# Moving the norm-factor multiply of tiles 1 to 3 from VectorE to GpSimd at the edge between two layers

## The chip, the cores and the metric

The kernel runs on one core of a Trainium2 chip. The metric is the device time of one launch in microseconds, and the time of a kernel is the median over its runs. Beside the runs there is one profiled execution; every row shown below is of that one.

## What is computed

A decoder trunk of two layers over 512 tokens of width 1024. Each layer normalises its input, runs three mixers (Mamba-2 SSD, latent attention, block-sparse attention) over one input projection, adds their output, normalises again and adds a mixture of experts. Only the first norm of a layer matters here:

```python
def _rms(x):
    return (x * lax.rsqrt(jnp.mean(x * x, axis=-1, keepdims=True) + EPS))

hm = rms_norm(x, norm_mix_g[l]) * (1.0 + sc_m) + sh_m
proj = hm @ w_in[l]
```

The kernel folds `norm_mix_g * (1 + sc_m)` into one row of factors, held in all 128 partitions in `mod[:, D:2*D]`. So a row of the norm's result is (x times factors) times rstd plus shift.

## The kernel before, in words

The 512 tokens are T = 4 tiles of 128 rows; `x[:, t, :]` is tile t, 128 partitions by 1024 f32. At the head of each layer `mixer_rows` (VectorE) makes the normed rows tile by tile. For a tile t the work is handed over as follows:

- ScalarE squares tile t and sums the squares along the row (`x_squares`, L1416, semaphore `xss`). In its own program this stands behind the copies of the columns of tile t-1 (`columns_out`, L1436).
- GpSimd makes rstd of the sum in two tiny instructions, a tensor_scalar (L2441) and a power (L2442), with a wait between them, and raises `xrs`.
- VectorE multiplies the tile by the factors into `x_scaled` (L1875, which is the whole buffer `gain`), once the row of t-1 that read this buffer is done (`hrow_dn`), and then, when `xrs` is up, makes the row: `x_scaled` times rstd plus shift (L1882, raises `hrow_dn`).
- TensorE turns the row into columns (L891), ScalarE copies them out of PSUM rounded to fp32r (L1436), and VectorE takes what the rounding left (`h_low`, L1841). TensorE then multiplies the tile with the first block of input weights (L953). It turns the columns of tile t+1 in the middle of tile t's 24 matmuls, so the rows of the next tile are wanted early.

After tile 3 the further blocks of the projection (L951, L953) follow without a break, whose first operand is all columns of all four tiles.

At the head of the second layer the tiles of x aren't final yet. VectorE adds what the experts gave: `added` (L1767, two of 128x512 for a tile, PSUM and x) and `chosen_added` (L1782, 128x1024, two for a tile, with gathered rows in SBUF and x). In `mixer_rows` these stand between the steps above: for a tile t, `added` of tile t+2, the multiply of tile t, the first `chosen_added` of tile t+1, the row of tile t, the second `chosen_added` of t+1, and `h_low` of t. ScalarE's squares of a tile wait for the second `chosen_added` of it.

GpSimd's own program has nothing else in this stage, apart from the gathers of chosen rows ahead of tile 0 in the second layer, and a memset and one DMA behind tile 3 in the first. Its loop over the tiles before the change is:

```python
for t in range(T):
    g.wait_ge(*at(L, xss, t + 1))
    rstd(rs_x[:, t:t + 1], ss_x[:, t:t + 1], D, xrs)
```

SyncE's loads that hang on this stage are those of the second input block (after row 0) and the first pieces of `ada_w` (after row 2, and after the last transposed columns).

Of the kernel before, what the change touches and what calls it, by code (L numbers as in the profile page):

```python
# [24 lines left out]
ALU = mybir.AluOpType  # L25
# [3 lines left out]
S, D, DEPTH = 512, 1024, 2  # L29
# [83 lines left out]
def trunk(nc, A, out, cpack, bucket_oh, relv, hf_rows, y_rows, mod_rows):  # L113
# [4 lines left out]
    def sb(name, shape, dt=F32):  # L118
        address[name] = -(-nc.sbuf_base // 32) * 32
        return ctx.enter_context(nc.sbuf_tensor(name, shape, dt))  # L120
# [5 lines left out]
    def sem(name, count=0):  # L126

        sems.append(ctx.enter_context(nc.semaphore(name)))
        per_layer[sems[-1].num] = count
        return sems[-1]  # L130

    def at(layer, sem_, n):

        assert n == 0 or per_layer[sem_.num] >= n
        return sem_, n + layer * per_layer[sem_.num]


    x = sb("x", [P, T, D])
    mod = sb("mod", [P, 6 * D])
# [75 lines left out]
    def h_row(base, t):  # L215
        return hfrow[:, t, :] if base else hrow[:, t % 2, :]
# [13 lines left out]
    x_scaled = gain[:]  # L230
# [128 lines left out]
    g_used = sem("gain_used", 5)  # L359
    hrow_dn = sem("h_row_done", 12)  # L360
# [342 lines left out]
    if True:  # L703
        with nc.Block() as block:
# [1056 lines left out]
            def _(v):  # L1761
# [7 lines left out]
                def added(L, t):  # L1769

                    for b in range(2):
                        v.wait_ge(ov_pe[L], TOKEN_ORDER.index((b, t)) + 1)
                        add_by_token(0, b, t).then_inc(x_added, 1)

                def chosen_added(L, t, j):

                    if j == 0:
                        v.wait_ge(*at(L, x_added, 2 * t + 2))
                        v.wait_ge(*at(L, cg[t], 32))
                    else:  # L1780
                        v.wait_ge(vch, step.n)
                    ins = v.scalar_tensor_tensor(x[:, t, :], chosen[:, 2 * t + j, :], w12[:, j, t:t + 1],  # L1782
                                                 x[:, t, :], ALU.mult, ALU.add)
                    if j:
                        ins.then_inc(cdn, 1)
                    else:
                        ins.then_inc(vch, 1)
                        step.n += 1

                def layer(L):  # L1790
# [46 lines left out]
                    def h_low(t):  # L1837

                        for j in range(2):
                            v.wait_ge(*at(L, h_ev, 2 * t + j + 1))  # L1840
                            v.tensor_tensor(hL[:, 4 * j:4 * j + 4, P * t:P * t + P],  # L1841
                                            h_bank(0, t, j)[:, :].rearrange("p (k n) -> p k n", k=4),
                                            actT_r[:, 4 * j:4 * j + 4, P * t:P * t + P].bitcast(F32), ALU.subtract
                                            ).then_inc(hl_dn, 1)

                    def in_weights_lo(i, halves=(0, 1)):
                        for half in halves:
                            raw, lo, hi = in_part(IN_ORDER[i], half)
                            v.wait_ge(*at(L, in_w_hi, 2 * i + half - 1))
                            v.tensor_tensor(lo, raw, hi.bitcast(F32), ALU.subtract).then_inc(in_w_lo, 1)  # L1850
# [9 lines left out]
                    def mixer_rows():  # L1860

                        g_ = mod[:, D:2 * D]
                        if L:
                            added(L - 1, 0)
                            added(L - 1, 1)
                            chosen_added(L - 1, 0, 0)
                            chosen_added(L - 1, 0, 1)
                        for t in range(T):
                            if L:
                                v.wait_ge(*at(L - 1, cdn, t + 1))  # L1870
                                if t + 2 < T:
                                    added(L - 1, t + 2)
                            if t:
                                v.wait_ge(*at(L, hrow_dn, t))
                            v.tensor_tensor(x_scaled, x[:, t, :], g_, ALU.mult).then_inc(g_used, 1)  # L1875
                            if L and t < T - 1:
                                chosen_added(L - 1, t + 1, 0)
                            v.wait_ge(*at(L, xrs, t + 1))
                            v.wait_ge(*at(L, g_used, t + 1))
                            if t >= 2:  # L1880
                                v.wait_ge(*at(L, h_ps, 2 * (t - 1)))
                            v.scalar_tensor_tensor(h_row(0, t), x_scaled, rs_x[:, t:t + 1], mod[:, 0:D], ALU.mult, ALU.add  # L1882
                                                   ).then_inc(hrow_dn, 1)
                            if L and t < T - 1:
                                chosen_added(L - 1, t + 1, 1)
                            if t == T - 1:
                                in_weights_lo(1, halves=(0,))
                            h_low(t)

                    def ffn_rows():  # L1890
# [6 lines left out]
                        for t in range(T):  # L1897
# [13 lines left out]
                            if t < T - 1:  # L1911
                                w_out_add(t + 1, 1)

                    mixer_rows()
                    in_weights_lo(1, halves=(1,))

# [255 lines left out]
                    for n in range(4 * T, 8 * T):  # L2172
                        h, t = n // T, n % T
# [261 lines left out]
            def _(g):  # L2435
                step = Counted(g, gch)
                def layer(L):

                    def rstd(dst, src, width, done):

                        step(g.tensor_scalar(dst, src, 1.0 / width, EPS, ALU.mult, ALU.add))  # L2441
                        g.tensor_tensor(dst, dst, cst[:, C_HALF:C_HALF + 1].to_broadcast(list(dst.shape)), ALU.pow  # L2442
                                        ).then_inc(done, 1)
# [7 lines left out]

                    for t in range(T):
                        g.wait_ge(*at(L, xss, t + 1))
                        rstd(rs_x[:, t:t + 1], ss_x[:, t:t + 1], D, xrs)

                    if L == 0:
# [162 lines left out]
                for L in range(DEPTH):  # L2619
                    layer(L)  # L2620
# [31 lines left out]
```

## Time and profile before

| | us |
|---|---|
| median of 3 runs | 1408.68 |
| lowest and highest run | 1405.8 and 1413.34 |
| profiled execution, its time | 1411.56 |
| profiled execution, its span | 1409.7 |
| TensorE busy in the span | 1312.8 (93%) |
| VectorE busy | 1130.7 (80%) |
| ScalarE busy | 731.6 (52%) |
| GpSimd busy | 237.3 (17%) |

The span is what the profile shows of the program from its first to its last record; 1.86 us of the execution's time lie around it. The mean granted clock of TensorE was 0.972 of full speed. Busy shares are averages over stages: which engine sets the time at the head of a layer has to be read from the timeline of that stage.

### The profile page before, as it was taken

What the parts mean: (1) busy time and instruction counts of PE and PEld (TensorE: products, weight loads), DVE (VectorE), ACT (ScalarE), POOL (GpSimd) and SP (SyncE); (2) the same over time, 40 slices, a digit from 0 to 9 for tenths busy, and PEclk for the clock granted to TensorE, in tenths of its full rate; (3) what the DMA queues carried; (4) which work ended last, traced back from release to release, by engine and by line L of the source; (5) the groups of instructions that cost most, each with busy time, mean ns of one, the idle gap of its engine ahead of it and who ended that gap; (6) DMA issues with size and microseconds to landing.
All of it is one profiled execution on the core that took longest, in us unless ns stands there. A gap on an engine that the chain in (4) does not pass through costs nothing.

```text
span 1409.7 us, 16989 instructions
## 1 busy us (share of the span) xinstructions
PE 1312.8 (93%) x6515; PEld 1045.8 (74%) x6515; DVE 1130.7 (80%) x1335; ACT 731.6 (52%) x963; POOL 237.3 (17%) x293
## 2 busy tenths in 40 slices
PE   6799988879989999999999998988998999999995
PEld 3677766667878888888877777666777888888883
DVE  3679867875579999999886998475557999999986
ACT  1424334562337777777624343447223877777760
POOL 0100136431011000000030013445101100000002
PEclk9899998999999999999999999899999999999998
DMA  9686621433579999999766583010347999999965
GB/s 358 244 297 216 224 94 61 149 119 121 212 292 360 411 409 409 406 407 411 263 229 209 171 277 124 1 60 1 150 173 286 369 403 408 401 415 406 405 238 194
DMA packets 90147, 365.93 MB, mean 260 GB/s; under 512 B 5785, under 2 KB 10631, under 8 KB 80464
## 3 DMA queue, kind: packets, MB, share of 16 engines
q1 hardware_dynamic: 67584, 298.71, 55.7%
q0 software_dynamic: 14160, 51.43, 9.4%
q10 hardware_dynamic: 8320, 14.68, 3.0%
q8 instruction: 53, 0.87, 0.2%
q14 instruction: 30, 0.25, 0.1%
HBM read 336.18 MB, written 28.61 MB: 259 GB/s over the span
## 4 chain that ended last, share of the span: by engine, by line
PE 76%; DVE 10%; issue 4%; ACT 3%; POOL 2%; DMA 2%; DVEq 0%; ACTq 0%; POOLq 0%
PE ps L953 9%; PE ps L1302 8%; PE ps L1304 8%; PE ps L1303 8%; PE ps L951 6%; PE ps L1330 4%; PE ps L1331 4%; PE ps L1332 4%; PE ps L1224 2%; PE ps L1226 2%; PE ps L1225 2%; PE ps L1288 2%; PE ps L1095 1%; PE ps L1126 1%; PE ps L920 1%
## 5 line engine op out<-in xcount | busy, mean ns | idle before, releaser
L1302 PE MATMUL ps<-mod_rounded,work_rounded 128*128 128x512 f32 x340 | 136.9, 403 | 1.8 <-DVE work_rounded L2345 1.8
L1304 PE MATMUL ps<-mod_rounded,work_rounded 128*128 128x512 f32 x340 | 134.6, 396 | 0.0
L1303 PE MATMUL ps<-ring_rounded,work_rounded 128*128 128x512 f32 x288 | 113.9, 396 | 0.0
L2204 DVE TENSOR_TENSOR ring_rounded<-ring,mod_rounded 128x2048 fp32r<-128x2048 f32 (+1 forms) x54 | 102.8, 1929 | 1.4
L1303 PE MATMUL ps<-work_rounded 128*128 128x512 f32 x256 | 101.0, 395 | 0.0
L2204 DVE TENSOR_TENSOR work_rounded<-work,mod_rounded 128x2048 fp32r<-128x2048 f32 (+1 forms) x48 | 91.3, 1930 | 10.0 <-ACT mod_rounded L1680 8.8
L2587 POOL DMA_INDIRECT work<-ffn_rows,slot_idx x34 | 42.0, 1235 | 302.0 <-PE ps L1288 269.3
L953 PE MATMUL ps<-ring_rounded,actT_rounded 128*128 128x512 f32 (+2 forms) x256 | 91.1, 356 | 0.0
L1680 ACT ACTIVATE mod_rounded<-ring 128x2048 fp32r<-128x2048 f32 (+1 forms) x54 | 85.9, 1626 | 0.0
L1812 DVE SCALAR_TENSOR_TENSOR gain<-ring,csil,gain 128x512 f32<-128x512 f32 x106 | 80.8, 763 | 3.0
L1700 ACT ACTIVATE work_rounded<-ps 128x512 fp32r<-128x512 f32 x68 | 37.0, 596 | 84.5 <-PE ps L1288 84.5
L1304 PE MATMUL ps<-actT_rounded,work_rounded 128*128 128x512 f32 x204 | 80.4, 394 | 0.0
L1302 PE MATMUL ps<-actT_rounded,work_rounded 128*128 128x512 f32 x204 | 80.1, 392 | 0.0
L953 PE MATMUL ps<-work_rounded,mod_rounded 128*128 128x512 f32 (+2 forms) x192 | 74.3, 387 | 2.4 <-ACT work L1443 1.3
L1680 ACT ACTIVATE mod_rounded<-work 128x2048 fp32r<-128x2048 f32 (+1 forms) x48 | 76.3, 1624 | 0.0
L1302 PEld LDWEIGHTS ps<-mod_rounded,work_rounded 128*128 128x128 f32 x340 | 64.1, 188 | 16.3 <-DVE work_rounded L2345 2.7
L1304 PEld LDWEIGHTS ps<-mod_rounded,work_rounded 128*128 128x128 f32 x340 | 63.9, 188 | 14.8
L2204 DVE TENSOR_TENSOR ring_rounded<-ring,actT_rounded 128x3072 fp32r<-128x3072 f32 x18 | 60.4, 3356 | 12.2 <-ACT actT_rounded L1680 12.2
L953 PE MATMUL ps<-work_rounded,actT_rounded 128*128 128x512 f32 (+2 forms) x192 | 70.0, 365 | 0.0
L2602 POOL DMA_DIRECT2D expert_rows<-work x32 | 18.1, 567 | 298.5 <-DVE work L2339 298.5
L1303 PEld LDWEIGHTS ps<-ring_rounded,work_rounded 128*128 128x128 f32 x288 | 54.3, 189 | 12.5
L2204 DVE TENSOR_TENSOR work_rounded<-work,actT_rounded 128x3072 fp32r<-128x3072 f32 x16 | 53.7, 3358 | 12.3 <-ACT actT_rounded L1680 12.2
(367 smaller groups left out, 3600.9 us busy)
## 6 DMA issues: line engine op xcount, KB each, us to landing
ring<-in_moe_w_up SPq DMA_DIRECT2D x18, 2048.0 KB, 10.7
ring<-in_moe_w_gate SPq DMA_DIRECT2D x18, 2048.0 KB, 10.4
ring<-in_moe_w_down SPq DMA_DIRECT2D x18, 2048.0 KB
work<-in_moe_w_up SPq DMA_DIRECT2D x16, 2048.0 KB, 10.8
work<-in_moe_w_down SPq DMA_DIRECT2D x16, 2048.0 KB, 11.5
work<-in_moe_w_gate SPq DMA_DIRECT2D x16, 2048.0 KB, 10.4
ring<-in_ada_w SPq DMA_DIRECT2D x30, 1024.0 KB, 5.3
expert_rows<-work POOLq DMA_DIRECT2D x32, 512.0 KB, 7.8
```

The costliest lines, as they stand in the source:

```text
L951: mm = pe.matmul(ps[n % 2][:, :], w_[:, P * t:P * t + P], h_, start=first_, stop=last_)
L953: mm = pe.matmul(ps[n % 2][:, 0:wd], h_[:, P * t:P * t + P], w_, start=first_, stop=last_)
L1302: pe.matmul(ps[j][:, :], xl, hi, start=k == 0, stop=False)
L1303: pe.matmul(ps[j][:, :], xh, lo, start=False, stop=False)
L1304: mm = pe.matmul(ps[j][:, :], xh, hi, start=False, stop=k == KD - 1)
L1330: pe.matmul(ps[6 + b][:, :], hl[:, k, :], hi_[:, k - k0, cols], start=k == 0, stop=False)
L1331: pe.matmul(ps[6 + b][:, :], hh[:, k, :], lo_[:, k, cols], start=False, stop=False)
L1332: mm = pe.matmul(ps[6 + b][:, :], hh[:, k, :], hi_[:, k - k0, cols], start=False, stop=k == 3)
L1680: a.activation(buf, slots[3 * odd + j][:, 512 * k0:512 * k1], ACT.Copy).then_inc(w_hi, 1)
L1812: add(v.scalar_tensor_tensor(acc, w, csil[:, k:k + 1], acc, ALU.mult, ALU.add))
L2204: v.tensor_tensor(slots_r[3 * odd + j][:, 512 * k0:512 * k1], slots[3 * odd + j][:, 512 * k0:512 * k1], buf.bitcast(F32), ALU.subtract).th ...
L2587: g.indirect_dma_start(out=dst, out_offset=None, in_=hf_rows, in_offset=bass.IndirectOffsetOnAxis(ap=col, axis=0)).then_inc(sem_, 16)
```

## The change

The multiply of tile 0 stays on VectorE. For tiles 1, 2 and 3 it is taken out of VectorE's program together with its wait for the row before, and put into GpSimd's loop, behind the wait for the squares and ahead of rstd. It happens at the head of both layers. Buffers, semaphores and counts are the same.

```diff
@@ -1870,9 +1870,8 @@
                                 v.wait_ge(*at(L - 1, cdn, t + 1))
                                 if t + 2 < T:
                                     added(L - 1, t + 2)
-                            if t:
-                                v.wait_ge(*at(L, hrow_dn, t))
-                            v.tensor_tensor(x_scaled, x[:, t, :], g_, ALU.mult).then_inc(g_used, 1)
+                            if t == 0:
+                                v.tensor_tensor(x_scaled, x[:, t, :], g_, ALU.mult).then_inc(g_used, 1)
                             if L and t < T - 1:
                                 chosen_added(L - 1, t + 1, 0)
                             v.wait_ge(*at(L, xrs, t + 1))
@@ -2451,6 +2450,9 @@
 
                     for t in range(T):
                         g.wait_ge(*at(L, xss, t + 1))
+                        if t:
+                            g.wait_ge(*at(L, hrow_dn, t))
+                            g.tensor_tensor(x_scaled, x[:, t, :], mod[:, D:2 * D], ALU.mult).then_inc(g_used, 1)
                         rstd(rs_x[:, t:t + 1], ss_x[:, t:t + 1], D, xrs)
 
                     if L == 0:
```

## Rows read from the trace of the kernel before

**Rows 1.** The page: busy time of each engine.

```profile
PE 1312.8 (93%) x6515; PEld 1045.8 (74%) x6515; DVE 1130.7 (80%) x1335; ACT 731.6 (52%) x963; POOL 237.3 (17%) x293
```

**Rows 2.** Windows: stretch and length, PE, PEld, DVE, ACT, POOL busy, clock, DMA, GB/s.

```profile
46.00:52.00 6.00, 5.59 (x26) 5.62 (x27) 2.85 (x4) 1.84 (x4) 0.76 (x2) 0.50 0.04 8
...
57.30:63.10 5.80, 5.71 (x36) 5.26 (x33) 3.71 (x4) 2.12 (x5) 1.45 (x2) 1.00 0.74 277
...
729.00:736.00 7.00, 4.93 (x34) 4.36 (x32) 6.56 (x9) 2.12 (x4) 0.74 (x2) 1.00 0.98 348
...
84.00:186.00 102.00, 102.00 (x483) 82.57 (x482) 95.99 (x127) 38.77 (x65) 10.08 (x7) 1.00 0.59 203
```

**Rows 3.** The chain of waits in the first layer, one tile: start, us, what.

```profile
58.21 1.04 ACT work L1416 x2
...
59.33 0.91 POOL sml L2441
...
60.30 0.56 POOL sml L2442
...
60.89 1.30 DVE work L1882
...
62.23 0.67 PE ps L891 x4
```

**Rows 4.** The timeline of the first layer's head: start, us, engine, line, operation.

```profile
47.63 0.19 POOL L2441 TENSOR_SCALAR sml<-sml 128x1 f32<-128x1 f32 x1 [47.20 <-ACT work L1416]
...
53.62 0.78 POOL L2441 TENSOR_SCALAR sml<-sml 128x1 f32<-128x1 f32 x1 [5.15 <-ACT work L1416]
...
55.08 1.28 DVE L1882 SCALAR_TENSOR_TENSOR work<-gain,sml,mod 128x1024 f32<-128x1024 f32 x1 [0.72 <-POOL sml L2442]
...
58.96 1.22 DVE L1875 TENSOR_TENSOR gain<-x,mod 128x1024 f32<-128x1024 f32 x1
...
65.55 0.48 POOL L2441 TENSOR_SCALAR sml<-sml 128x1 f32<-128x1 f32 x1 [4.69 <-ACT work L1416]
...
66.69 1.28 DVE L1882 SCALAR_TENSOR_TENSOR work<-gain,sml,mod 128x1024 f32<-128x1024 f32 x1 [0.72 <-POOL sml L2442]
```

**Rows 5.** The timeline of the second layer's head, tiles 1 to 3.

```profile
731.35 0.19 POOL L2441 TENSOR_SCALAR sml<-sml 128x1 f32<-128x1 f32 x1 [5.16 <-ACT work L1416]
...
733.43 1.28 DVE L1782 SCALAR_TENSOR_TENSOR x<-work,sml,x 128x1024 f32<-128x1024 f32 x1
...
734.62 1.28 DVE L1882 SCALAR_TENSOR_TENSOR work<-gain,sml,mod 128x1024 f32<-128x1024 f32 x1
...
738.86 0.89 POOL L2441 TENSOR_SCALAR sml<-sml 128x1 f32<-128x1 f32 x1 [6.68 <-ACT work L1416]
...
741.34 1.29 DVE L1882 SCALAR_TENSOR_TENSOR work<-gain,sml,mod 128x1024 f32<-128x1024 f32 x1 [0.44 <-POOL sml L2442]
...
746.00 0.48 POOL L2441 TENSOR_SCALAR sml<-sml 128x1 f32<-128x1 f32 x1 [4.69 <-ACT work L1416]
...
747.15 1.28 DVE L1882 SCALAR_TENSOR_TENSOR work<-gain,sml,mod 128x1024 f32<-128x1024 f32 x1 [0.72 <-POOL sml L2442]
```

**Rows 6.** GpSimd's multiplies by line: count, ns min/median/max, first and last start, shape.

```profile
L2482 POOL TENSOR_TENSOR work<-work,hpar x8: 1042/1049/1071, 190.8 to 934.7; 128x512 f32<-128x512 f32 x8
...
L2488 POOL TENSOR_TENSOR ring<-work,sml x16: 612/623/1434, 186.4 to 925.3; 128x256 f32<-128x256 f32 x16
```

**Rows 7.** VectorE and GpSimd side by side in the mixers of the first layer.

```profile
L2029 DVE TENSOR_TENSOR work<-work x16: 671/686/1337, 192.8 to 943.7; 128x512 f32<-128x512 f32 x16
...
258.62 0.83 POOL L2488 TENSOR_TENSOR work<-actT,sml 128x384 f32<-128x384 f32 x1
258.66 1.34 DVE L2029 TENSOR_TENSOR work<-work 128x512 f32<-128x512 f32 x1
...
277.75 2.29 DVE L2083 TENSOR_TENSOR ring_rounded<-ring,biasm_rounded 128x2048 fp32r<-128x2048 f32 x1
...
277.87 2.65 POOL L2488 TENSOR_TENSOR work<-mod,sml 128x256 f32<-128x256 f32 x1
```

## The prediction, made before the changed kernel ran

> **What bounds the kernel now.** I began with the page. TensorE is busy 93% of the span, VectorE 80%, GpSimd 17% [rows 1]. That invites the thought that moving VectorE work to GpSimd is free. It says nothing about the stage touched, so I read next the windows of the two layer heads, then the chain through them, then the timeline.
>
> In the first layer's head a tile takes 5.80 us, TensorE busy 5.71 of it and VectorE only 3.71 [rows 2]. The chain there does not stay on TensorE: ScalarE's squares, GpSimd's two tiny instructions, VectorE's row, TensorE's transposes, ScalarE's column copies, and again squares [rows 3]. What the reader should see is that GpSimd's rstd is in this ring, and VectorE's multiply is not: it runs from 58.96 to 60.18 while the squares end and rstd begins [rows 4]. TensorE is nearly full as well, but it follows the ring: the transposes start 0.04 us after the row ends. Behind the stage TensorE is busy 102.00 of 102.00 us [rows 2], so there is no hole in which a later row 3 could be made good.
>
> One more thing stands in the timeline. The first rstd instruction takes 0.19 us for tile 0, but 0.78, 0.91 and 0.48 us for tiles 1 to 3 [rows 3, 4]. The one at 59.33 ends at 60.22 or so, just behind the multiply that VectorE ends at 60.18. So while VectorE runs an instruction with two inputs in SBUF, GpSimd's reading instruction stands still. It holds the other way too: VectorE's 128x512 add of two SBUF tiles has a median of 686 ns and a longest of 1337 ns [rows 7], and one of 1.34 us started at 258.66, just behind GpSimd's 0.83 us multiply at 258.62 [rows 7]. GpSimd's 128x256 multiply, 0.62 us alone [rows 6], took 2.65 us from 277.87, beside a VectorE instruction that ran to 280.04 [rows 7]. Each waits for the whole instruction of the other.
>
> **The change, step by step.**
>
> *Removed from VectorE:* six multiplies of 1.22 us [rows 4], and their waits for the row before. In the first layer this was beside ScalarE and GpSimd work, and what it costs the ring is only the stall it puts on rstd. In the second layer VectorE is busy 6.56 of 7.00 us around tile 1 [rows 2] and the multiply of tile 1 delays what follows on VectorE.
>
> *Added to GpSimd:* six multiplies of 128x1024, each between the end of the squares and rstd, the one place where nothing hides it. The wait for the row before costs nothing: rows 55.08 and 60.89 [rows 3, 4] are done 3 us before the next squares end. No transfer is queued behind it on GpSimd, except the first layer's zeroing memset and DMA behind tile 3, which move with the row. What is queued is rstd itself, and VectorE's row waits for that.
>
> *The size M of one multiply.* The trace has none of 1024. The nearest are 128x512 at 1.05 us and 128x256 at 0.62 us [rows 6], both with one operand read whole and one broadcast. Carrying the slope of their minima on (1042 less 612 over 256 elements, 1.68 ns each) gives 1.90 us, doubling the 128x512 gives 2.10. Here both operands are read whole, which speaks for the higher one, and the row of 512 is the nearer: I take M = 2.1. As bounds for the range I take 1.22, VectorE's own time for it [rows 4], below which nothing suggests it can go, and 2.5, four times the 128x256 median, where the whole fixed cost of an instruction is counted four times.
>
> The Trainium skill's page "GPSIMD Engine Reference", section "Elementwise — side-by-side cycle accounting", speaks against the change: it gives 4497 ns for such an add of 2048 elements on GpSimd against 2293 ns on VectorE. Half of that would be an estimate of 2.25 us, by which the sum below would come to +9.9 us instead of +9.0; no row here shows the operation.
>
> *First layer.* After the change the time from GpSimd's start to VectorE's row is M, then 0.08 gap, 0.19, 0.08 gap, 0.56 and 0.03: M + 0.94 = 3.04 us, rstd no longer stalled because VectorE has nothing with two SBUF inputs there. Before, it was 55.08 less 53.62 = 1.46, 60.89 less 59.33 = 1.56, 66.69 less 65.55 = 1.14 [rows 3, 4]. The differences are 1.58, 1.48 and 1.90: **+5.0 us**. The ring passes each on in full, as squares of the next tile stand behind this row's columns.
>
> *Second layer, tile 1.* GpSimd may start at 731.35 and holds the port to 733.45. VectorE, spared its multiply, comes to the first `chosen_added` of tile 2 at 732.3; it has two SBUF inputs and stands until 733.45, ending at 734.6. Rstd's first instruction waits for that, and the row starts at 735.34 instead of 734.62 [rows 5]: +0.72. *Tile 2.* The squares end 0.72 later, so GpSimd could start at 739.58 rather than 738.86 [rows 5]. But VectorE now reaches the first `chosen_added` of tile 3 at 739.2, ahead of it, and holds the port to 740.4. Multiply and rstd then bring the row to 743.4 against 741.34: +2.1 in all. *Tile 3.* Nothing else runs on VectorE; GpSimd starts at 746.00 + 2.1, and 3.04 later the row starts, 751.1 against 747.15 [rows 5]: **+4.0 us** in all.
>
> The sum is 5.0 + 4.0 = +9.0 us; as a formula in M, 6M less 3.65, so each 0.1 us of M is 0.6 us. Against the profiled execution's own 1411.56 (span 1409.7 and 1.86 around it) that is 1420.6. That execution is 2.9 above the median 1408.68, so as a median I forecast **1417.7**. Two costs I set to nothing: the added wait instructions on GpSimd (it is idle, and they run before the squares end) and SyncE's loads behind row 2 and the last columns. The loads go out 3 to 5 us later, but their reader, VectorE's first ada sum, is held until then by a transposed parameter tile behind the same rows. If that cover were gone, it would be those 3 to 5 us.
>
> **The rivals.**
>
> *A cheaper multiply.* The place is the same six multiplies, the price 6M less 3.65. From M = 1.78 down the kernel is no longer slower by 0.5% (7.0 us), which is about what a measurement of this kernel can tell from no change. At VectorE's speed, 1.22, the cost is +3.7: **1412.4**; at 1.5 it is +5.4. For it: between 256 and 512 elements the time does not double, 1.68 ns an element [rows 6] is already near, and a plain pattern may run faster than a broadcast one. Against it: even the slope gives 1.90. Within this bound also lies some unnamed slack later in a layer that takes up 2 us or more of 9. I give this 0.28 with the scatter of runs, 1405.8 to 1413.34, counted in.
>
> *TensorE's clock falls.* After the change a tile takes about 7.3 us with 5.7 of TensorE work. If the clock fell to 0.50, the 1.2 GHz level that it has from 46 to 52 us [rows 2], a tile's 5.7 us of TensorE work would take 11.4, 4 us more than its period; for two tiles, +8 more: **1426**. Against it: around tile 1 of the second layer TensorE is busy 4.93 of 7.00 us and the clock stayed at 1.00, the 2.4 GHz level [rows 2]. I give it 0.05.
>
> *The multiply hides and the kernel gets faster.* Were GpSimd's multiply to run ahead of the squares' end, the stalls of rstd (0.6, 0.7, 0.3 in the first layer, 0.7 on the first instruction of tile 2 and 0.3 of tile 3 in the second) and the 1.2 us of VectorE at tile 1 would go: 3.8 us less, **1404.9**. It would decide if GpSimd started a multiply over 2.1 us before the end of the squares. The order of the waits excludes it, since the wait for `xss` is first. 0.02. That the multiply doesn't move at all, as a no-op rival, is excluded by the diff.
>
> **How the numbers follow.** The forecast with M from 1.85 to 2.5 (+7.5 to +11.4) has 0.65, the cheaper multiply or slack 0.28, the clock 0.05, the gain 0.02. Slower by over 0.5% is 0.65 + 0.05, less 0.04 for scatter that pulls a +8 under the bound: 0.66. Within is 0.32, and faster 0.02. The range reaches down to 1411.0, the cheap multiply with 1.4 us of scatter, and up to 1424.0, the dear multiply (+11.4, 1420.1) with most of the 4.7 us by which the highest run stands over the median.
>
> **What would show it.** In the changed profile: six GpSimd multiplies of gain<-x,mod, of about 2.1 us, the two of tile 2 and perhaps 1 in the second layer longer by a wait on VectorE; rstd's first instruction at 0.19 us in the first layer; the distance from GpSimd's start to the row 3.0 us; the period between rows 7.2 us in place of 5.8; VectorE idle before L1882 by 3 us, for GpSimd; a first `chosen_added` of about 2.3 us in the second layer; row 3 at 71.7 and at 756.1 (5.0 of the first layer and 4.0 of its own) by the old clock of the span; from there on every start late by a constant. The forecast is wrong if M is under 1.8, if rows 3 are late as forecast but the end is not, or if the granted clock drops in either head.

## The result, and the profile after

The changed kernel takes 1426.46 us (median of 8 runs, 1418.91 to 1433.78). The kernel before, run beside it, takes 1414.45 us over 8 runs, three of which are the ones known ahead of the prediction. The ratio is 1.0082, 95% interval [1.0056, 1.0107]: 0.8% slower, about 12 us. Forecast was slower by 9.0 us, 1417.7 us, with a range up to 1424.0. The direction holds, the time lies outside the range. Two of all executions that follow, one of the kernel before (2455.56 us) and one of the first-layer-only kernel (2349.49 us), are far off the rest and stand in no ratio.

The profiled execution of the changed kernel took 1421.47 us, its span is 1419.7 us, 10.0 more than before. From the page, the busy time of each engine, to be laid beside [rows 1]:

```profile
PE 1313.1 (92%) x6515; PEld 1048.4 (74%) x6515; DVE 1125.3 (79%) x1329; ACT 731.6 (52%) x963; POOL 249.4 (18%) x299
```

VectorE lost 5.4 us of work and six instructions, GpSimd gained 12.1 us, TensorE did the same as before. These sums do not say where the 10.0 us come from; the timeline does. The first layer's head in the changed kernel, against [rows 3, 4]:

```profile
53.91 2.39 POOL L2455 TENSOR_TENSOR gain<-x,mod 128x1024 f32<-128x1024 f32 x1 [5.14 <-ACT work L1416]
56.38 0.19 POOL L2440 TENSOR_SCALAR sml<-sml 128x1 f32<-128x1 f32 x1
```

```profile
48.80 1.28 DVE L1881 SCALAR_TENSOR_TENSOR work<-gain,sml,mod 128x1024 f32<-128x1024 f32 x1 [0.80 <-POOL sml L2441]
...
57.24 1.28 DVE L1881 SCALAR_TENSOR_TENSOR work<-gain,sml,mod 128x1024 f32<-128x1024 f32 x1 [3.73 <-POOL sml L2441]
...
72.77 1.29 DVE L1881 SCALAR_TENSOR_TENSOR work<-gain,sml,mod 128x1024 f32<-128x1024 f32 x1 [4.03 <-POOL sml L2441]
```

GpSimd starts when the squares end, multiplies for 2.39 us, and only then makes rstd. VectorE stands idle for 3.73 and 4.03 us ahead of a row where it stood 0.72 before. The first rstd instruction takes 0.19 us, as forecast: its stall of 0.3 to 0.7 us is gone. I call the time from the start of row 0 to the start of row 3 the head. It is 72.77 - 48.80 = 23.97 us, against 18.18 before (66.69 of [rows 4], less 48.51, row 0's start). The first head contains one thing that the multiply doesn't touch: the transposes of row 0, which took 1.92 us here and 1.91 in the kernel before, with the granted clock at 0.50. In other profiles the clock rises earlier, and they take down to 1.09 us. So first heads differ by up to 0.8 us for this alone, whatever the kernel, and where it matters below I give the time of these transposes.

The second layer, against [rows 5]:

```profile
741.68 2.37 POOL L2455 TENSOR_TENSOR gain<-x,mod 128x1024 f32<-128x1024 f32 x1 [4.90 <-ACT work L1416]
744.13 1.05 POOL L2440 TENSOR_SCALAR sml<-sml 128x1 f32<-128x1 f32 x1
...
750.08 3.15 POOL L2455 TENSOR_TENSOR gain<-x,mod 128x1024 f32<-128x1024 f32 x1 [4.27 <-ACT work L1416]
```

```profile
737.46 1.27 DVE L1881 SCALAR_TENSOR_TENSOR work<-gain,sml,mod 128x1024 f32<-128x1024 f32 x1
...
742.63 2.50 DVE L1782 SCALAR_TENSOR_TENSOR x<-work,sml,x 128x1024 f32<-128x1024 f32 x1
...
749.72 1.28 DVE L1782 SCALAR_TENSOR_TENSOR x<-work,sml,x 128x1024 f32<-128x1024 f32 x1
...
762.62 1.29 DVE L1881 SCALAR_TENSOR_TENSOR work<-gain,sml,mod 128x1024 f32<-128x1024 f32 x1 [4.22 <-POOL sml L2441]
```

Here both engines want the port, the thing that they share and for which one waits while the other's instruction runs. VectorE's add at 742.63 takes 2.50 us instead of 1.28, as GpSimd multiplies until 744.05; rstd's first instruction then takes 1.05 us, until just after that add ends at 745.13. One tile later the order is reversed: the add starts at 749.72, before GpSimd's 750.08, and it is the multiply that takes 3.15 us instead of 2.4. The head is 25.16 us against 20.29 (747.15 less 726.86).

So the two heads lose 5.79 + 4.87 = 10.66 us. The stages, each between starts of TensorE's instructions of a line, weight loads where nothing else is said (head: first weight load to last matmul of L891; projection: from there to the first of L972; mixers: to the first of L1224; output and router: to the first of L1280; experts: to the next layer's first of L891, or the end of the span), show what lies elsewhere. The two lower lines are profiles of the same two kernels taken again:

```
us                1st layer: head  proj.  mixers  output  experts   2nd layer: head  proj.  mixers  output  experts
before                       19.1  115.6   133.3    74.8    335.8              20.9  115.6   125.1    75.5    344.2
changed                      24.8  115.6   136.4    74.8    337.1              26.0  115.6   120.6    75.5    343.2
before, again                18.7  115.6   134.3    74.8    336.3              21.0  115.5   122.4    74.9    343.7
changed, again               25.4  116.2   133.9    74.9    336.1              25.7  115.5   122.1    75.5    343.1
```

The loss of the heads is passed on by the projections, which are within 0.6 us of each other in all four. The mixers change their length by some us from one execution to the next, in either kernel.

### The profile page after: what moved, and what is told of

Read it like the earlier page. It is cut to its first block, busy times and chain, and to the rows that moved or that the text cites. A ratio compares the mean times of both kernels' runs of the same rounds, so it can differ in the third digit from the quotient of the medians.

```text
span 1419.7 us, 16994 instructions
## 1 busy us (share of the span) xinstructions
PE 1313.1 (92%) x6515; PEld 1048.4 (74%) x6515; DVE 1125.3 (79%) x1329; ACT 731.6 (52%) x963; POOL 249.4 (18%) x299
## 4 chain that ended last, share of the span: by engine, by line
PE 72%; DVE 10%; issue 6%; ACT 4%; POOL 3%; DMA 2%; DVEq 0%; ACTq 0%; POOLq 0%
PE ps L953 9%; PE ps L1304 8%; PE ps L1302 8%; PE ps L1303 8%; PE ps L951 6%; PE ps L1331 4%; PE ps L1330 4%; PE ps L1332 4%; PE ps L1224 2%; PE ps L1226 2%; PE ps L1225 2%; PE ps L1288 2%; PE ps L1095 1%; PE ps L1126 1%; PE ps L882 1%
## 5 line engine op out<-in xcount | busy, mean ns | idle before, releaser
L2203 DVE TENSOR_TENSOR ring_rounded<-ring,actT_rounded 128x3072 fp32r<-128x3072 f32 x18 | 60.4, 3356 | 12.1 <-ACT actT_rounded L1680 12.1
L2203 DVE TENSOR_TENSOR work_rounded<-work,actT_rounded 128x3072 fp32r<-128x3072 f32 x16 | 53.7, 3358 | 12.3 <-ACT actT_rounded L1680 12.1
```

The lines of the kernel that those rows point to most:

```text
L2203: v.tensor_tensor(slots_r[3 * odd + j][:, 512 * k0:512 * k1], slots[3 * odd + j][:, 512 * k0:512 * k1], buf.bitcast(F32), ALU.subtract).th ...
```

## The experiments

A ratio is the time of the kernel over that of the kernel before, run beside it (13 to 29 runs), with its 95% interval. Each kernel has 8 to 12 runs where nothing else is said. The heads are read from one profiled execution of each.

**The multiply moved in one layer only.** The condition `if t` of GpSimd's block becomes `if t and L == 0`, or `L == 1`, and VectorE keeps the other layer's:

```diff
-                            if t == 0:
+                            if t and L != 0:
+                                v.wait_ge(*at(L, hrow_dn, t))
+                            if t == 0 or L != 0:
                                 v.tensor_tensor(x_scaled, x[:, t, :], g_, ALU.mult).then_inc(g_used, 1)
...
-                        if t:
+                        if t and L == 0:
```

> The multiplies of tiles 1 to 3 go to GpSimd in the first layer only. Head of a layer means the time from the start of row 0 to the start of row 3 (kernel before: 18.18 us in the first layer, 20.29 us in the second; changed kernel: 23.97 and 25.16). Ring theory (GpSimd's multiply of 2.39 us stands whole between the squares and rstd, and nothing later takes it up): heads of 24.0 and 20.3 us, 5.8 us more than before, ratio about 1.004. Clock rival (most of the loss comes from a lower granted clock that the changed head sets off later): the mixers of the first layer are again some 3 us longer than before, and the time goes up by clearly more than the head.

Measured: heads of 23.14 and 20.03 us; ratio 1.0064 [1.0036, 1.0092]. The 0.8 us that the first head lacks to 24.0 are row 0's transposes, 1.10 us here.

> The multiplies of tiles 1 to 3 go to GpSimd in the second layer only. Ring theory: heads of 18.2 us in the first layer and 25.2 us in the second, 4.9 us more than before, ratio about 1.0035; with the first-layer-only kernel's 5.8 us it adds up to the 10.7 us of both heads. Slack rival (VectorE, freed of its multiply, gives something back in the second layer, where it is the busier one): second head under 23.5 us.

Measured: heads of 18.19 and 25.48 us; ratio 1.0068 [1.0041, 1.0095]. Each head behaves as the ring theory says, alone as in both together, and VectorE gives nothing back in the second layer. But each kernel loses 9 to 10 us where its head loses about 5, and the two together 18.6 us, where both heads changed at once cost 12. In the first one the profile has the rest in the mixers of the first layer, 142.3 us long against 133.3. That is taken up again below.

**The multiply done twice.**

```diff
                             g.wait_ge(*at(L, hrow_dn, t))
+                            step(g.tensor_tensor(x_scaled, x[:, t, :], mod[:, D:2 * D], ALU.mult))
                             g.tensor_tensor(x_scaled, x[:, t, :], mod[:, D:2 * D], ALU.mult).then_inc(g_used, 1)
```

> As the changed kernel, but GpSimd does each multiply of tiles 1 to 3 twice, the second waiting for the first. Ring theory: each of the six tiles takes 2.39 + 0.08 us more, so heads of about 31.4 and 32.6 us (the second within 1 us, as the port is taken in another order), and some 14.8 us more than the changed kernel, about 25.5 us over the kernel before, ratio 1.018. Slack rival: less than 10 us over the changed kernel. Clock rival: TensorE idles 4 us of each tile, the clock falls in the heads, and the heads grow by clearly more than 7.4 us each.

Measured: heads of 32.14 and 33.55 us, so 8.2 and 8.4 us more than in the changed kernel; ratio 1.0186 [1.0118, 1.0254] from 4 runs, some 26 us. There is no slack in the ring, to twice the dose. The 0.8 and 1.0 us a head beyond 7.4 go with the clock, which was at 0.50 from 60 to 66 us: the transposes of row 1 took 1.97 us in the first head instead of 1.09, and those of rows 1 and 2 took 1.87 and 1.97 us in the second.

**GpSimd multiplies before it waits for the squares.**

```diff
                     for t in range(T):
-                        g.wait_ge(*at(L, xss, t + 1))
                         if t:
                             g.wait_ge(*at(L, hrow_dn, t))
+                            if L:
+                                g.wait_ge(*at(L - 1, cdn, t + 1))
                             g.tensor_tensor(x_scaled, x[:, t, :], mod[:, D:2 * D], ALU.mult).then_inc(g_used, 1)
+                        g.wait_ge(*at(L, xss, t + 1))
```

> GpSimd keeps the multiplies, but does each before it waits for the squares (after the row before, and in the second layer after the tile's last added row). Ring theory: the place costs, not the engine. First head: 18.18 less the rstd stalls of 1.6, about 16.6 us. Second head: the multiply of 2.4 us ends about when the squares do, about 19.3 us. So 2.5 us less than before and 13 less than the changed kernel. Rival (GpSimd's multiply costs wherever it stands, as it holds the port against VectorE): second head at 22 us or more.

Measured: heads of 17.21 and 19.77 us, both shorter than before, though by 0.6 and 0.5 us less than expected; ratio 0.9987 [0.9949, 1.0024], no measurable change. Its first layer, on GpSimd:

```profile
55.67 2.39 POOL L2456 TENSOR_TENSOR gain<-x,mod 128x1024 f32<-128x1024 f32 x1 [1.40 <-DVE work L1881]
58.77 0.19 POOL L2440 TENSOR_SCALAR sml<-sml 128x1 f32<-128x1 f32 x1 [0.70 <-ACT work L1416]
```

The same 2.39 us, now with 0.70 us of idle time behind them until the squares end. This is the experiment that decides: GpSimd does the same six multiplies at the same speed, and the loss of 10.7 us is gone. It was the place behind the wait, not the engine.

Why the first head gains 1.0 us and not 1.6 stands in the windows. Row 2 is ready at 60.91 us, but TensorE starts its transposes only at 61.42, and those of row 3 come 5.50 us later. TensorE is busy throughout:

```profile
61.40:66.90 5.50, 5.50 (x33) 5.23 (x32) 2.65 (x4) 4.34 (x6) 3.81 (x5) 1.00 0.89 306
```

So with the ring shortened TensorE itself sets the pace between rows 2 and 3, at 5.5 us where the ring took 5.8. In the second layer the multiply held up an add of VectorE, which took 2.24 us instead of 1.28.

**What sets the size of one multiply.** First, each multiply cut in two halves of 128x512:

```diff
-                            g.tensor_tensor(x_scaled, x[:, t, :], mod[:, D:2 * D], ALU.mult).then_inc(g_used, 1)
+                            g.tensor_tensor(x_scaled[:, 0:512], x[:, t, 0:512], mod[:, D:D + 512], ALU.mult)
+                            g.tensor_tensor(x_scaled[:, 512:D], x[:, t, 512:D], mod[:, D + 512:2 * D], ALU.mult).then_inc(g_used, 1)
```

> As the changed kernel, but each GpSimd multiply of 128x1024 is two of 128x512. If the time of a multiply is a fixed part of about 0.18 us and 2.16 us per 1024 elements, a half takes 1.26 us. If the elements are cheap and the fixed part is large, a half takes 1.4 us or more. If two full operands cost no more than one full and one broadcast, a half takes the 1.05 us of the skip product and the pair beats 2.39 us.

Second, the whole length, but with a second operand that is broadcast:

```diff
-                            g.tensor_tensor(x_scaled, x[:, t, :], mod[:, D:2 * D], ALU.mult).then_inc(g_used, 1)
+                            g.tensor_tensor(x_scaled.rearrange("p (h n) -> p h n", h=16), x[:, t, :].rearrange("p (h n) -> p h n", h=16),
+                                            mod[:, D:D + 16].unsqueeze(2).to_broadcast([P, 16, HP]), ALU.mult).then_inc(g_used, 1)
```

> As the changed kernel, but the second operand of GpSimd's multiply is 16 of the factors, each broadcast over 64 elements, instead of the 1024 factors: the norm's factors are not applied rightly in tiles 1 to 3. Theory (a full second operand is read element by element and is what made 2.1 us too low): the multiply takes 1.90 to 2.1 us, and the first head is 23.97 less three times the difference, about 22.8 us. Rival (only the length counts, the slope from shorter rows was misleading): 2.39 us again.

Each of these two has a single execution, of 1426.98 us (halves) and 1416.65 us (broadcast), so only their profiles are used. Measured, the lines of the multiply in the changed kernel, in the one of halves (two rows) and in the one of the broadcast operand (count, ns min/median/max):

```profile
L2455 POOL TENSOR_TENSOR gain<-x,mod x6: 2366/2396/3154, 53.9 to 759.2; 128x1024 f32<-128x1024 f32 x6
```

```profile
L2455 POOL TENSOR_TENSOR gain<-x,mod x6: 1267/1295/2047, 52.9 to 763.8; 128x512 f32<-128x512 f32 x6
L2456 POOL TENSOR_TENSOR gain<-x,mod x6: 1277/1283/2267, 54.2 to 765.0; 128x512 f32<-128x512 f32 x6
```

```profile
L2455 POOL TENSOR_TENSOR gain<-x,mod x6: 1902/1904/2677, 52.9 to 749.6; 128x1024 f32<-128x1024 f32 x6
```

With a broadcast operand 1024 elements take 1.904 us, which is where the slope of [rows 6] pointed (1.90). With two full operands it is 2.396 us, and 1.29 for half of it, so (2.396 - 1.29) / 512 = 2.16 ns an element and some 0.18 us fixed. The fixed part is the same as that of the broadcast rows (1.042 less 512 times 1.68 ns); a second operand that is read whole costs 0.48 ns more an element. The broadcast run handles all three operands in groups of 64 elements, as the rows of 512 do; what the pattern does apart from the broadcast isn't separated. The first heads are 21.78 us with the broadcast operand and 23.73 with halves. Three multiplies shorter by 0.49 us, or longer by 0.15 (a pair of halves takes 2.54 us from start to end), make 22.5 and 24.4 of 23.97; the rest, some 0.7 us, is row 0's transposes, 1.12 and 1.17 us in these two profiles.

**Idle matmuls while TensorE waits.**

```diff
                                 if i == 0 and k == 4 and t < T - 1:
+                                    keep_warm(12)
                                     to_columns(t + 1)
```

> As the changed kernel, but TensorE does 12 idle matmuls of 128x128 (some 1.3 us) into a free bank ahead of the transposes of tiles 1 to 3 in both heads, in the time in which it waits for the row. In the changed kernel the granted clock fell to 0.50 between 60 and 62 us. Ring theory: the clock dip sits under TensorE's own waiting and costs nothing, so the heads stay at 24.0 and 25.2 us within 0.3 us, and the time at that of the changed kernel. Clock rival: the clock stays at 1.00 in the head and the first head shrinks by 1 us or more.

Measured: heads of 23.92 and 25.44 us; ratio 1.0100 [1.0073, 1.0127] from 4 runs. One window of the changed kernel and the same of this one (length, PE, PEld, DVE, ACT, POOL busy, granted clock, DMA, GB/s):

```profile
60.00:62.00 2.00, 2.00 (x7) 1.85 (x7) 1.20 (x2) 1.40 (x3) 0.52 (x1) 0.50 0.34 126
```

```profile
60.00:62.00 2.00, 2.00 (x12) 1.93 (x12) 0.16 (x1) 0.36 (x2) 1.56 (x1) 1.00 0.51 186
```

The clock is at its upper level of 2.4 GHz (1.00) and the head gains nothing, but this doesn't decide. Two other things cancel in the head: row 0's transposes took 1.09 us here and not 1.92, and the idle matmuls ran 0.8 us over the arrival of row 2. And the first-layer-only kernel, whose first head is the same code, had 1.00 from 60 to 62 us without any idle matmul:

```profile
60.00:62.00 2.00, 2.00 (x12) 1.94 (x11) 0.26 (x1) 0.46 (x2) 1.47 (x1) 1.00 0.68 242
```

This kernel makes the comparison: its rows 1 and 2 are 7.56 us apart, those of the changed kernel, with the fall to 0.50 between them, 7.54. So that fall cost nothing.

Is a fall of the clock in the head always free, then? No. From the chain of waits in the changed kernel, and then in its second profile:

```profile
58.59 0.67 PE ps L891 x4
```

```profile
58.24 1.94 PE ps L891 x8
```

In the second the transposes of row 1 ran at the lower level, 1.2 GHz, and the distance from row 1 to row 2 was 8.35 us, not 7.54. So the fall costs where it meets the transposes, which are on the ring, and nothing where it meets the matmuls behind them. The first heads of the changed kernel and of the first-layer-only kernel, 23.1 to 24.6 us in four profiles, spread for this: 23.14 with the transposes of rows 0 and 1 both at 1.1 us, 23.97 with those of row 0 at 1.92, 24.63 and 24.51 with those of row 1 at 1.9 as well and those of row 0 at 1.75 and 1.56.

**VectorE's multiply moved up.** The other way to keep it off rstd, in the kernel before:

```diff
-                            if t:
-                                v.wait_ge(*at(L, hrow_dn, t))
-                            v.tensor_tensor(x_scaled, x[:, t, :], g_, ALU.mult).then_inc(g_used, 1)
+                            if t == 0:
+                                v.tensor_tensor(x_scaled, x[:, t, :], g_, ALU.mult).then_inc(g_used, 1)
...
                                 chosen_added(L - 1, t + 1, 1)
+                            if t < T - 1:
+                                v.wait_ge(*at(L, hrow_dn, t + 1))
+                                if L:
+                                    v.wait_ge(*at(L - 1, cdn, t + 2))
+                                v.tensor_tensor(x_scaled, x[:, t + 1, :], g_, ALU.mult).then_inc(g_used, 1)
```

> The kernel before, with VectorE's multiply of tile t+1 moved up to just behind the row of tile t (in the second layer behind the tile's last added row), ahead of the low part of the columns. Theory (in the kernel before, the multiply stood in the way of rstd through the shared port): first rstd instruction 0.19 us for all tiles, first head 18.18 - 1.6 = 16.6 us, second head about 19.0 us, 2.9 us less than before, ratio 0.998. Rival (the stall of rstd is no port matter but the start of an idle engine): rstd's first instruction still 0.5 to 0.9 us, heads unchanged.

Measured: heads of 16.33 and 19.11 us; ratio 0.9988 [0.9957, 1.0018], by itself no measurable change. Its first layer, on GpSimd and on VectorE:

```profile
58.81 0.19 POOL L2445 TENSOR_SCALAR sml<-sml 128x1 f32<-128x1 f32 x1 [4.28 <-ACT work L1416]
```

```profile
55.88 1.23 DVE L1889 TENSOR_TENSOR gain<-x,mod 128x1024 f32<-128x1024 f32 x1
```

The multiply fills the hole in which VectorE waits for the columns, and all eight first rstd instructions take 0.19 us. GpSimd was idle for 4.28 us ahead of this one, as long as ahead of the stalled one before, so the stall was not the start of an idle engine: it was VectorE's multiply running beside it. The Trainium skill's page "SBUF — State Buffer", section "Who interferes with whom", says that a VectorE instruction with two inputs in SBUF contends with a GpSimd instruction that reads SBUF, and that one with at most one input there (outside its two-port modes) does not. The traces agree on both. For the second, `h_low`, with one input in PSUM, started while GpSimd's multiply ran, from 55.67 to 58.06 us, in the kernel that multiplies before the squares, and neither took longer for it (1.29 and 2.39 us, as alone):

```profile
57.19 1.29 DVE L1841 TENSOR_TENSOR mod_rounded<-ps,actT_rounded 128x512 fp32r<-128x512 f32 x2 [1.60 <-ACT actT_rounded L1436]
```

The same kernel with more runs:

> The kernel with VectorE's multiply moved up behind the row before, with more runs. From its heads (16.3 and 19.1 us, 3.0 us less than the kernel before together) the ratio should be 0.9979; if the gain is eaten elsewhere it is 1.000.

Measured: heads of 16.36 and 19.11 us; ratio 0.9982 [0.9964, 0.9999]. The heads are 3.0 us shorter, 0.2%, but up to 0.7 us of it is row 0's transposes (1.18 and 1.20 us in these two profiles, 1.91 in the kernel before), which this edit doesn't touch. The measured 0.18% is just clear of no change. It is the one arrangement here with such a result, in one of its two measurements. As above, TensorE sets the pace at the end of the first head: it is busy for all of the 5.50 us between the transposes of rows 2 and 3.

**A delay that has nothing to do with GpSimd.** In the kernel before, two idle squares on ScalarE ahead of the real one of tiles 1 to 3:

```diff
+                        if t and not after_w_out:
+                            for _ in range(2):
+                                step(a.activation(square, x[:, t, :], ACT.Square))
                         a.activation(view(4096, D) if after_w_out else square, x[:, t, :], ACT.Square,
```

> The kernel before, with no multiply moved, but ScalarE does two idle squares of 128x1024 (about 1.06 us each, with a wait for each) ahead of the real one of tiles 1 to 3 in both heads: some 2.3 us on the ring by another engine. Ring theory: any 2.3 us there cost the same; since VectorE's multiply is then over before rstd starts, the rstd stall goes, so the heads are about 18.2 + 6.9 - 1.6 = 23.5 us and 20.3 + 3.2 to 5, about 24.5 us, some 10 us more, ratio 1.007. Rival (the loss came from GpSimd and VectorE sharing the port, not from the place on the ring): heads grow by under 3 us each, ratio under 1.004.

Measured: heads of 23.58 and 23.56 us, so 5.4 and 3.3 us more than before; ratio 1.0048 [1.0021, 1.0074]. Some 2.2 us of work of another engine in the same place lengthen the heads too, with no multiply moved. The time alone doesn't exclude the rival's 1.004; the heads do, each longer by over 3 us. The first head has row 1's transposes at 1.97 us in it, so part of its match is luck. The second head lost 0.9 us less than expected, and the time 2 us less than its heads, within the interval.

**Both kernels again.**

> The kernel before, unchanged, against itself. Ratio 1.000 within its interval. Scatter theory (the mixers between the input projection and the output projection change their length from one execution to the next, by the granted clock, whatever the kernel): heads again 18.2 and 20.3 us and the projections within 0.2 us of 115.6, but the mixers of the first layer differ from the 133.3 us of the first profile by 1 us or more. Rival (each kernel has its own fixed mixer length, so the changed kernel's 136.4 us is a cost of the change): again 133.3 us.

Measured: ratio 0.9999 [0.9975, 1.0022], heads of 17.94 and 20.31 us, mixers of 134.3 and 122.4 us (133.3 and 125.1 in the first profile). The same kernel differs by 1.0 and 2.7 us in its mixers.

> The changed kernel, unchanged, with more runs. Ring theory: ratio near 1.0075 (10.7 us of the two heads on 1413), heads 23.1 to 24.0 and 25.2 us. Rival (the change also lengthens the mixers by lowering the clock there): ratio 1.010 or more, with the mixers of the first layer again 136 us or more.

Measured: ratio 1.0075 [1.0052, 1.0098] from 6 runs, heads of 24.63 and 24.80 us, mixers of 133.9 and 122.1 us. With the mixers as long as the other kernel's, the loss is that of the heads: 6.5 + 4.5 = 11.0 us, or 0.78%.

**One layer at a time, again.**

> First layer only, again, with more runs. If the 4 us beyond the head in the first measurement were scatter of the granted clock: ratio 1.003 to 1.005, and the mixers of the first layer anywhere between 131 and 138 us. If a shifted head lowers the clock in the mixers: ratio 1.0065 or more again, and the mixers of the first layer near 142 us again.

Measured: heads of 24.51 and 20.02 us, mixers of 137.0 us; ratio 1.0078 [1.0051, 1.0105].

> Second layer only, again, with more runs. Scatter: ratio 1.003 to 1.005. A loss behind the head: ratio 1.0065 or more again. The mixers of the first layer lie ahead of this kernel's change, so a longer length there can't be its doing.

Measured: heads of 17.81 and 24.77 us, mixers of 135.5 us, which lie ahead of the change; ratio 1.0047 [1.0025, 1.0068]. This is 6.6 us, with an interval from 3.5 to 9.6, beside the 4.5 us of its head. The first layer alone lost 11.0 us beside the 6.3 of its head. In all four measurements the layers taken singly lose more than their heads, by 2 to 5 us, and their sums, 18.6 and 17.7 us, are well over the 12 and 10.6 us of the full change.

The excess goes with the mean granted clock of the runs. Its median is 0.965 to 0.968 in these four, 0.969 and 0.970 in the two measurements of the changed kernel, and 0.971 to 0.973 in those of the kernel before. Where the clock is lost shows in the windows over the mixers of the first layer. The kernel before, and the first-layer-only kernel's first profile (granted clock third from the end):

```profile
186.00:330.00 144.00, 122.55 (x677) 90.59 (x676) 106.70 (x193) 73.28 (x181) 60.85 (x77) 0.92 0.38 129
```

```profile
192.00:336.00 144.00, 121.83 (x639) 89.82 (x637) 99.77 (x189) 71.03 (x178) 58.92 (x76) 0.86 0.34 114
```

The first-layer-only kernel's second profile has 0.89. But so has the second-layer-only kernel's first, with mixers of 137.1 us that lie ahead of any change, and the kernel with VectorE's multiply moved up, whose head is shorter, has 0.87 and 137.7 us in its second profile. The changed kernel itself has 0.88 in its first profile and 0.92 in its second. So a low clock in these mixers is no mark of a shifted head; the ScalarE delay, which shifts the first head as much, has 0.92 and mixers of 133.0 us. Over the sixteen profiles of this case these mixers take 131.4 to 142.3 us, the shortest at 0.93 and the longest at 0.86. Why the medians of the single-layer kernels are higher than their heads explain stays open.

## Why the prediction was right in its mechanism and wrong in its time

*What bounds the stage.* Right. The ring through GpSimd's rstd was the bound in both heads, nothing behind the heads took the loss up, and TensorE merely followed. The doubled multiply, the ScalarE delay and the multiply ahead of the wait show it from three sides. What I hadn't seen is how near the next bound lies: TensorE's own 5.5 us a tile.

*The size M of one multiply.* This term was mis-sized: 2.1 us in the sum, 2.39 measured. The rows of before all had a broadcast operand. I saw that, took the doubling of the 128x512 row as allowance for it, and fell 0.3 us short; six times that is 1.7 us. The estimate of 2.25 us, half of the figure in the Trainium skill's page "GPSIMD Engine Reference", section "Elementwise — side-by-side cycle accounting", was nearer, and 0.15 short as well. The formula itself held: 6 times 2.39 less 3.65 is 10.7 us, and the heads lost 10.66. By layer it gives 5.8 and 4.9; measured were 5.79 and 4.87. That the second layer fits to a few hundredths is luck, as told below.

*First layer.* Rstd unstalled, 0.19 us for each tile, as forecast. From GpSimd's start to the row it is 57.24 - 53.91 = 3.33 us, which is M + 0.94 with the measured M. The distances between rows were 8.44, 7.54 and 7.99 us. My own terms give 8.15, 7.29 and 7.70, so each is over by the 0.29 us of M; the 7.2 that I gave as the period holds for the middle one at most.

*Second layer.* The two port waits came as told: the add of tile 2 held up by the multiply (2.50 us against a forecast of 2.3), the multiply of tile 2 held up by the add of tile 3 (3.15 us). The rows lost 0.63, 1.60 and 2.64 us against my 0.72, 1.4 and 1.9. With M at 2.39 my terms would be 1.0, 1.7 and 2.2: the first came out 0.4 us lower, as the squares of tile 1 ended 0.27 us sooner after row 0 and that wait was shorter, and the last 0.4 us higher, as TensorE's transposes of row 2 took 1.53 us, at the lower clock, instead of 1.09. The two cancel.

*The level it was set on.* This is the step that failed and made the time miss the range. I put the 9.0 us on 1408.68, the median of three runs. The kernel before is 1414.45 with five more runs, 5.8 us higher, and 1412.7 to 1415.3 in the four later sets of 13 to 29 runs. On 1414.45 the forecast is 1423.4 even with M = 2.1, and the range moved up with it, 1416.8 to 1429.8, holds the measured time. On the old level it is 1419.4 with M right, and the measured time is outside. With both right the forecast is 1425.2, 1.3 us from the measured 1426.46. The range, 1411 to 1424, had let the upper run scatter in only once, for the dear multiply, and had nothing for the median of three lying low, though those three spread over 7.5 us.

*The rivals.* The cheaper multiply fell, and no slack showed. The hidden multiply that makes the kernel faster was rightly excluded by the order of the waits; put ahead of the wait, it came to 1.5 us less in the heads, where I had said 3.8, for one thing because TensorE became the bound. The clock rival was right that the clock falls in the changed heads (0.50 from 60 to 62 us and from 756 to 758), which I had thought unlikely from the second layer's head. I had named such a fall as a sign that the forecast is wrong, and it is a poor one, as the falls cost so little. Its price was wrong: up to 0.9 us where the fall meets the transposes, not 4 us a tile, since the matmuls that slow down lie in TensorE's waiting time.

*SyncE's loads and the added wait* cost nothing that shows: the projections are 115.6 us in both kernels, and 116.2 in one of four profiles of the table.

## What to carry to other kernels

Before giving work to an idle engine, ask whether that engine has an instruction on the chain at that point, and on which side of its wait the work goes: the same six multiplies lengthened the heads by 10.7 us behind the wait and shortened them by 1.5 us ahead of it. A small instruction on the chain can be stalled by a long one of the engine that shares its port, so a long one belongs into a hole in which nobody waits for either. And a forecast of a few per mille stands on the baseline as much as on the sum: a median of three runs was 0.4% off, half of the measured effect. And where a stage elsewhere in the kernel changes its length by as much as the effect from one execution to the next, measure the stage that you changed, not only the whole.

## What the runs showed of the hardware that I had not expected

GpSimd's multiply of two whole f32 operands takes 2.16 ns an element, with one operand broadcast 1.68 (2.396 against 1.904 us for 128x1024), so a row with a broadcast operand is no measure for one without. The mixers of the first layer took 131.4 to 142.3 us in sixteen profiles of kernels that are all the same there, with a granted clock of 0.93 to 0.86; what sets the clock in an execution stays open. The same transposes of row 0, ahead of everything that was changed, took 1.09 to 1.92 us.
